# The first attention block: ScalarE copies both halves of the output bank and GpSimd adds them

## The reference, cut to what matters

```python
def one_block(qblk):                      # 128 queries
    s = jnp.einsum('bqkgd,bskd->bkgqs', qblk, k).astype(jnp.float32)
    p = jax.nn.softmax(s, axis=-1).astype(v.dtype)
    return jnp.einsum('bkgqs,bskd->bqkgd', p, v)
o = lax.map(one_block, qb)
...
mix = jnp.concatenate([att, pool], axis=-1) @ w_out[l]
x = x + g1 * mix
```

## Time and profile before

| what | value |
|---|---|
| median of three runs | 2446.69 us (2444.95 to 2446.87) |
| the profiled execution | 2446.65 us, span 2444.9 us |
| PE busy | 2327.3 us (95%) |
| DVE busy | 1115.9 us (46%) |
| ACT busy | 774.1 us (32%) |
| POOL busy | 862.1 us (35%) |
| first attention | from about 201 to 424 us of the span |
| the exponentials, line 1275 | 64 of 1116 ns |
| scaling and extreme, line 1833 | 64 of 1287 ns |

### The profile page before, as it was taken

How to read it: one execution, slowest core, us unless ns; L and a number is a source line. 1 busy time by engine, 2 the same in 40 slices (tenths; PEclk the granted TensorE clock), 3 DMA queues, 4 the chain that set the end, 5 groups by cost and what they waited for, 6 DMA issues and landing times.

```text
span 2444.9 us, 30807 instructions
## 1 busy us (share of the span) xinstructions
PE 2327.3 (95%) x11310; PEld 1924.3 (79%) x11310; DVE 1115.9 (46%) x1405; ACT 774.1 (32%) x1095; POOL 862.1 (35%) x851
## 2 busy tenths in 40 slices
PE   4898888999999999999999999999999999999998
PEld 3676777878888888888777888888788888888886
DVE  7977887479631344123463334353311122222224
ACT  3236776032310232024424445362112111212210
POOL 1345554335333233323223333332223334333331
PEclk9999999999999999999999999999999999999998
DMA  7311001525111111111131111101111111111132
GB/s 308 105 55 35 17 26 56 212 103 174 50 52 43 52 49 45 52 61 43 39 116 64 38 55 46 45 30 65 34 39 51 43 47 61 43 47 47 43 129 78
DMA packets 48318, 164.84 MB, mean 67 GB/s; under 512 B 4480, under 2 KB 6272, under 8 KB 48128
## 3 DMA queue, kind: packets, MB, share of 16 engines
q1 hardware_dynamic: 48256, 164.02, 20.4%
HBM read 155.61 MB, written 8.39 MB: 67 GB/s over the span
## 4 chain that ended last, share of the span: by engine, by line
PE 78%; DVE 11%; issue 5%; ACT 4%; POOL 1%; DMA 0%; DVEq 0%; ACTq 0%; SPq 0%; POOLq 0%
PE acc L752 60%; PE turn L989 6%; PE bank L1053 3%; DVE ADA L1677 2%; DVE acc L1833 1%; PE bank L1031 1%; PE acc L977 1%; ACT EX L1275 1%; PE turn L646 1%; PE acc L730 1%; PE acc L688 1%; DVE HL L1657 1%; PE bank L1127 1%; DVE CV L1965 1%; PE bank L866 1%
## 5 line engine op out<-in xcount | busy, mean ns | idle before, releaser
L752 PE MATMUL acc<-HH,WH 128*128 128x512 f32 x1584 | 491.5, 392 | 4.8 <-POOL WL L544 2.5
L752 PE MATMUL acc<-HL,WH 128*128 128x512 f32 x1584 | 488.8, 390 | 0.0
L752 PE MATMUL acc<-HH,WL 128*128 128x512 f32 x1584 | 488.5, 390 | 0.0
L541 POOL TENSOR_TENSOR WH<-WF,CON 128x16 fp32r<-128x16 f32 x186 | 52.3, 281 | 1191.0 <-PE acc L752 1060.5
L544 POOL TENSOR_TENSOR WL<-WF,WH 128x1024 fp32r<-128x1024 f32 (+3 forms) x186 | 440.5, 2368 | 15.5
L752 PEld LDWEIGHTS acc<-HH,WH 128*128 128x128 f32 x1584 | 297.6, 188 | 69.1 <-ACT CV L1356 4.1
L752 PEld LDWEIGHTS acc<-HL,WH 128*128 128x128 f32 x1584 | 298.1, 188 | 62.4
L752 PEld LDWEIGHTS acc<-HH,WL 128*128 128x128 f32 x1584 | 297.9, 188 | 62.2
L542 POOL TENSOR_SCALAR WH<-WF 128x1008 fp32r<-128x1008 f32 (+3 forms) x186 | 193.1, 1038 | 0.0
L1965 DVE SCALAR_TENSOR_TENSOR CV<-EV,VEC,CV 128x1023 f32<-128x1023 f32 x44 | 94.1, 2139 | 202.3 <-ACT CV L1356 202.3
L1893 DVE SCALAR_TENSOR_TENSOR XT<-acc,MOD,XT 128x1024 f32 (+1 forms) x34 | 43.5, 1283 | 230.5 <-PE acc L752 230.5
(11 more groups left out here) (382 smaller groups left out, 4114.8 us busy)
## 6 DMA issues: line engine op xcount, KB each, us to landing
WF<-in_w SPq DMA_DIRECT2D x150, 512.0 KB, 3.6
ADA<-in_ada SPq DMA_DIRECT2D x15, 1024.0 KB, 13.1
BIAS<-in_bias SPq DMA_DIRECT2D x16, 576.0 KB, 3.8
XT<-in_xT SPq DMA_DIRECT2D x16, 512.0 KB, 10.1
ADA<-in_ada SPq DMA_DIRECT2D x4, 2048.0 KB, 11.8
ADA<-in_ada SPq DMA_DIRECT2D x3, 2560.0 KB, 9.3
WF<-in_w SPq DMA_DIRECT2D x24, 256.0 KB, 2.6
ADA<-in_ada SPq DMA_DIRECT2D x8, 512.0 KB, 3.6
```

Source lines behind the costliest of these rows:

```text
L541: pool.tensor_tensor(h[:, 0:FEW], f[:, 0:FEW], zero.to_broadcast([P, FEW]), ALU.add).then_inc(w_hi, 1)
L752: last = pe.matmul(acc[:, slot, HALF * c:HALF * c + HALF], w[slot][:, k, :], x[:, k, HALF * c:HALF * c + HALF], start=(k == 0 and w is WH ...
```

## The change

The addition goes from DVE to POOL. POOL works only on SBUF tiles in this kernel, so ACT copies both halves of `bank6` to SBUF: rows 0 to 63 to a new tile `OTOP`, rows 64 to 127 to `OTMP` as before. PE waits for ACT's copies (`otmp_ready`) before it writes `bank6` again, no longer for the addition. In POOL's queue the addition stands at units 5, 9 and 13 behind `normalise` and the stacking of queries, and at the turn ahead of `branch_second`. A new one-column copy on ACT ahead of the attention gives `otmp_ready` its first count. POOL waits for its own two additions (`o_first`, `o_ready`).

```diff
+        OTOP = at("OTOP", 84, [P, HALF])
...
 # GpSimd, attend
                         stack_queries(it, 2, u - 9, it * 32 + (2 * u + 6))
+                    if u % 4 == 1 and u > 1:
+                        gather_o(it, u // 4 - 1)
                     if u == 12:
                         branch_second(it, 0)
+                gather_o(it, 3)
                 branch_second(it, 1)
+
+            def gather_o(it, b):
+
+                pool.wait_ge(otmp_ready, it * 4 + (b + 2))
+                g = b % 2
+                o = OTOP[0:64, :].rearrange("p (i j q) -> p i j q", j=2, q=P)
+                m = OTMP[0:64, :].rearrange("p (i j q) -> p i j q", j=2, q=P)
+                if g == 0:
+                    pool.wait_ge(ml_ready, it * 2 + (b // 2 + 1))
+                pool.tensor_tensor(OT[0:64, 2 * g:2 * g + 2, :], o[:, :, 0, :], m[:, :, 0, :], ALU.add).then_inc(o_first, 1)
+                pool.wait_ge(o_first, it * 4 + (b + 1))
+                pool.tensor_tensor(OT[64:128, 2 * g:2 * g + 2, :], o[:, :, 1, :], m[:, :, 1, :], ALU.add).then_inc(o_ready, 1)
+                pool.wait_ge(o_ready, it * 4 + (b + 2))
...
 # TensorE, values
                     if c == 0:
-                        pe.wait_ge(o_ready, it * 4 + (b + 1))
+                        pe.wait_ge(otmp_ready, it * 4 + (b + 1))
...
 # ScalarE
                 act.wait_ge(o_ready, it * 4 + (b + 1))
+                act.activation(OTOP[0:64, :], bank6[0:64, :], ACT.Copy)
                 act.activation(OTMP[0:64, :], bank6[64:128, :], ACT.Copy).then_inc(otmp_ready, 1)
...
             act.wait_ge(post_done, TURN_AT[-1] + 1)
+            act.activation(SUM[:, 2:3], eps, ACT.Copy).then_inc(otmp_ready, 1)
             stack_queries(0, 0)
...
 # VectorE
-            def gather_o(it, b):
-
-                dve.wait_ge(otmp_ready, it * 4 + (b + 1))
-                g = b % 2
-                if g == 0:
-                    dve.wait_ge(ml_ready, it * 2 + (b // 2 + 1))
-                o = bank6[0:64, :].rearrange("p (i j q) -> p i j q", j=2, q=P)
-                m = OTMP[0:64, :].rearrange("p (i j q) -> p i j q", j=2, q=P)
-                link(dve.tensor_tensor(OT[0:64, 2 * g:2 * g + 2, :], o[:, :, 0, :], m[:, :, 0, :], ALU.add))
-                dve.tensor_tensor(OT[64:128, 2 * g:2 * g + 2, :], o[:, :, 1, :], m[:, :, 1, :], ALU.add).then_inc(o_ready, 1)
...
-                    if u % 4 == 1 and u > 1:
-                        gather_o(it, u // 4 - 1)
...
-                gather_o(it, 3)
...
-            with steps.loop(3, 4) as it:
+            with dve.Fori(0, 3) as it:
                 attend(it, False)
```

More of the change, by code:

```diff
@@ L305, in build @@
             sem("mh_ready"), sem("ml_ready"))
-        gated, gh_ready = sem("gated"), sem("gh_ready")
+        o_first, gated, gh_ready = sem("o_first"), sem("gated"), sem("gh_ready")
         silu_done = sem("silu_done")
```

## The result

The changed kernel took 2453.35 us, median of 9 runs (2451.58 to 2455.36), against 2447.32 us for 9 runs of the kernel before on the same chip. The ratio is 1.0024, 95% interval 1.0016 to 1.0033: slower, by 3.9 to 8.1 us. The forecast was 2452.6.

A forecast was written before the change was run, and what follows sets the result against it. PE bounds the program; in the attention DVE is fullest, but each place's awaited engine decides. -3.6 + 1.9 + 0.35 + 5.9 + 0.1 = 4.65, with 1.05 and 0.3 6.0, on 2446.65 gives 2452.6 us; range 2448.5 to 2457.5.

The forecast's parts named there:

- Units 5 and 13, with unit 13 of the last pass and the start: Eight places gain 0.45 us each, 3.6 less; last pass's unit 13 costs 0.35, the one-column copy ahead of the attention 0.1.
- Unit 9 with the meeting: Looped passes: ACT's copy at unit 9 costs 3 x 0.62 = 1.9 us; POOL's addition delaying `ADA` at unit 13, 1.05.
- POOL's late stacking: Behind unit 9, POOL's second stacking ends about 303.3, just when PE wants it for unit 13's scores; nothing charged.
- The turn: End of each pass, addition uncovered: `OTOP` to `MH` takes 3.09 us instead of 1.61, 4 x 1.48 = 5.9 more.
- The clock: PE idles 3.1 us at each turn and its clock falls; 0.1 charged for each of three turns, 0.3 in all.
- The signs: Expected in the profile after: turn 3.1 us, PE's wait 5.1, unit 5's `PTH` wait 0.4, longer exponential wait, longer `ADA`.
- no meeting: Rival, unit 13: POOL's additions come clear of `ADA`, or cost a little less than 0.74 us; 2451.3 us, chance 0.28.
- DVE's time in full: Rival, units 5, 9 and 13: DVE sets the pace, `PTH` is never late; 5.2 us less, 2441.5, chance 0.07.
- POOL's pace: Rival, from unit 9 on: additions of 1.0 us or more delay `MH` and unit 13's scores; 2456.1 us, chance 0.07.
- the clock's: Rival, each turn: PE's clock falls and PE gets late, up to 1.2 us a turn; 2455.9 us, chance 0.16.

The follow-up runs named there:

- The second set of runs: The changed kernel and the kernel before run again, no edit: changed 2453.66 us, ratio 1.0026; before 2448.39 us, ratio 0.9997.
- with only the copy: Kernel before, additions left on DVE, plus ACT's new copy of the lower half of `bank6`, read by nothing: 2452.40 us, ratio 1.0021.
- With `ADA` moved: Changed kernel with DVE's product `ADA` at units 6 and 14 instead of 5 and 13: 2452.73 us, ratio 1.0021 to the kernel before.

## Why the prediction held, step by step

The three steps between the kernels add up to the whole: units 5 and 13 alone (229.90 - 233.22 = -3.32), unit 9 added (232.45 - 229.90 = +2.55), the turn added (237.73 - 232.45 = +5.28), together +4.51.

- Units 5 and 13, with unit 13 of the last pass and the start: forecast -2.7 (seven times 0.45, less 0.35 and 0.1), measured -3.32. A place gives 0.5 to 0.6 and not 0.45, because the copy starts 0.1 us earlier than `OTMP` alone did, and DVE has no visible wait where I had set 0.4. The first pass gives only 0.2 at unit 5.
- Unit 9 with the meeting: forecast 1.9 + 1.05 - 0.45 = 2.5, measured 2.55. That these agree is luck, for three errors cancel. Unit 9 of a looped pass costs 0.44, as ACT is full (12.91 against 12.34 behind it, less 12.65 against 12.52 ahead), where I had 0.62. The way from unit 13 to the turn costs 0.61 (11.87 against 11.26), where I had 0.35: 0.53 for the meeting, and 0.08 for POOL's late stacking, for which I had charged nothing. Unit 9 of the last pass gives 0.6, where I had 0.45. `ADA` started 0.04 us behind POOL's first addition and took 0.55 longer; the second addition started while `ADA` ran and took 0.87 longer. These rows fit if each stood until the other was done: 313.07 + 1.21 = 314.28 for the end of `ADA`, and it ended at 314.15; 314.15 + 0.73 = 314.88 for the end of the second addition, and it ended at 314.74. The rule in the Trainium skill, SBUF — State Buffer, section "SBUF: two separate sides", that the second of the two is held for the whole instruction, agrees with these rows to 0.13 and 0.14 us.
- The turn: forecast 5.9, measured 5.28. The term was 1.48 and is 1.31: ACT hands over to POOL in 0.08 us and not in 0.19, and two copies take 1.20 from start to end and not 1.22. POOL's addition, taken as 0.74 halfway between bounds, is 0.73.
- The clock: forecast 0.3, measured 0. PE idled 2.74 us at a turn, where I had 3.1. The clock fell as the rival said, for some 4 us at each of three turns, and the slack held.
- The signs: PE's wait behind the attention is 5.05 us (forecast 5.1), a pass with its meeting is 1.2 longer (forecast 1.5), `MH` lies 2.92 behind `OTOP` (3.1). Two did not come: DVE shows no wait for `PTH` at unit 5 (0.4), and its wait for the exponential at unit 9 is 0.42 as before and not longer.

The sum of the attention was thus 1.5 us too high, mostly from the turn, the gain at units 5 and 13 and the clock. That the median still came within 0.8 us of the forecast is owed to what the 9 runs left open: the medians lie 6.0 us apart, and the attention's 4.5 us lies inside their interval of 3.9 to 8.1. That closeness is luck; the account place by place is not. The second set of runs put them 5.8 apart, so the other 1.5 us was there twice. Whether it is anything but the spread of the runs stays open; no trace shows it: outside the attention the two traces of before took 2211.7 and 2214.7 us, those of after 2214.6 and 2211.9.

Of the rivals, no meeting is refuted by the 1.76 us; DVE's time in full by ACT at unit 9; POOL's pace by 0.73, though the wait that it named, for the scores of unit 13, came in small (0.08 us a pass); the clock's by the distances. Its warning was right for another place: in the last pass a fall costs 1.2 us.

## What to carry to other kernels

Moving work to the emptiest engine paid here only where the last waiter waited for the engine relieved. The same edit gave 0.5 us where DVE was behind and cost 0.4 where ACT was full, 0.5 more where the moved work met DVE's own in SBUF, and 1.3 where three engines pass one result along; made at 8 of 16 places it won about 4 us, made at all 16 it lost 4 to 8. When an operation moves to another engine's queue, look at what stands ahead of it there and who waits for it, for that wait may have to move too: 11.9 us hung on the choice of one semaphore.

## What had not been expected

- The clock falls in one pass and not in another of the same kernel: with only the copy PE idled 2.21, 2.20 and 2.04 us at the three turns, and the granted clock in the 5 us behind was 1.00, 0.66 and 0.66. With `ADA` moved it was 1.00, 1.00 and 0.66, where after had 0.67, 0.66 and 0.67, all six behind 2.74 or 2.75 us of idle.
- Two instructions that meet can both be stretched, each by the other: `ADA` by 0.55 and the addition by 0.87 us.
- Profiles of unchanged code differ by up to 7 us in 2212, while the attention repeats to 0.03 where a kernel was traced twice (its first stretch was 0.8 us shorter in one of the twelve traces, where the clock stayed up longer). A change of a few microseconds is better read from its own stretch than from medians.
